# Head norms and value transposes moved into the query stage of a two-block transformer kernel on one Trainium2 core

## What is computed

```python
# block 1: local attention and pooling, then a gated FFN with a 3-tap convolution
z = rms_norm(x) @ w_in;  m = concat([attention, pool]) @ w_o;  x = x + rms_norm(m)
up = causal_dwconv(rms_norm(x) @ w_up);  y = (gelu(up_a) * up_b) @ w_down;  x = x + rms_norm(y)
# block 2: x and a context of 256 tokens, modulated by a condition vector
mods = silu(cond) @ w_ada + b_ada                       # six chunks of 2048, two for the context
kv = modulate(rms_norm(x or ctx)) @ w_in2[:, :3072]     # k_a, v_a (4 heads), k_b, v_b (8 heads)
p  = modulate(rms_norm(x)) @ w_in2[:, 3072:]            # q_a (16 heads), q_b (8 x 2), g_a, g_b
q, k = head_norm(q), head_norm(k);  both rotated (rope) for x, only normed for the context
oa = softmax(qa @ ka.T) @ va
ob = head_norm((softmax(qb0 @ kb0.T) - lam * softmax(qb1 @ kb1.T)) @ vb)
x = x + mod * ((sigmoid(g_a) * (oa @ w_br_a) + sigmoid(g_b) * (ob @ w_br_b)) @ w_out)
x = x + mod * ((silu(h @ w_ff_gate) * (h @ w_ff_up)) @ w_ff_down)
```

## Time and profile before

| what | us |
|---|---|
| runs of the kernel before | 3105.65, 3086.52, 3093.49 (median 3093.49) |
| the profiled execution, its own time | 3086.12 |
| its span, first to last instruction | 3084.3 |
| TensorE busy, weight loads aside | 2889.3 |
| VectorE, ScalarE, GpSimd busy | 1920.5, 1626.7, 806.3 |
| mean granted TensorE clock | 0.977 of 2.4 GHz |

### The profile page before, as it was taken

How to read it: one execution, slowest core, us unless ns; L and a number is a source line. 1 busy time by engine, 2 the same in 40 slices (tenths; PEclk the granted TensorE clock), 3 DMA queues, 4 the chain that set the end, 5 groups by cost and what they waited for, 6 DMA issues and landing times.

```text
span 3084.3 us, 57401 instructions
## 1 busy us (share of the span) xinstructions
PE 2889.3 (94%) x20282; PEld 2679.1 (87%) x20282; DVE 1920.5 (62%) x2324; ACT 1626.7 (53%) x2312; POOL 806.3 (26%) x646
## 2 busy tenths in 40 slices
PE   7998799899999997899999879989997999999999
PEld 7998799899999997788899769779996888888888
DVE  5566877866687766533355554657787665555554
ACT  5555566545577753323455566665555644344443
POOL 3454444403344422112242030004443400000000
PEclk9999899999999999999999889999998999999999
DMA  7873667667777775344476224348775876666665
GB/s 250 272 250 126 229 211 243 214 184 225 235 245 243 244 231 177 96 143 143 153 253 223 81 78 121 101 163 267 240 256 196 261 216 185 192 189 190 190 188 167
DMA packets 167990, 606.90 MB, mean 197 GB/s; under 512 B 18576, under 2 KB 19984, under 8 KB 167120
## 3 DMA queue, kind: packets, MB, share of 16 engines
q1 hardware_dynamic: 161856, 589.37, 60.7%
q10 hardware_dynamic: 5248, 13.30, 1.1%
q0 software_dynamic: 784, 2.88, 0.3%
HBM read 599.19 MB, written 6.29 MB: 196 GB/s over the span
## 4 chain that ended last, share of the span: by engine, by line
PE 67%; DVE 11%; ACT 9%; issue 6%; DMA 5%; ACTq 1%; DVEq 0%; SPq 0%
PE acc L1431 19%; PE acc L1427 14%; PE acc L1429 13%; PE acc L1430 12%; DVE wlo L918 4%; ACT whi L554 4%; DMA raw<-w_ada 3%; ACT cond_products L550 2%; PE acc L1419 1%; DVE conv_out L1006 1%; PE acc L1421 1%; PE acc L1422 1%; DMA raw<-w_up 1%; PE sums L1492 1%; PE acc L1639 1%
## 5 line engine op out<-in xcount | busy, mean ns | idle before, releaser
L918 DVE TENSOR_TENSOR wlo<-raw,whi 128x1024 fp32r<-128x1024 f32 x864 | 1131.7, 1319 | 952.3 <-ACT whi L554 950.6
L1431 PE MATMUL acc<-operand,wlo 128*128 128x256 f32 (+1 forms) x4992 | 1452.8, 291 | 0.0
L554 ACT ACTIVATE whi<-raw 128x1024 fp32r<-128x1024 f32 x864 | 908.5, 1057 | 942.2 <-PE acc L1431 616.1
L1429 PE MATMUL acc<-operand,whi 128*128 128x256 f32 (+1 forms) x3584 | 1073.8, 300 | 94.4 <-DVE wlo L918 58.4
L1430 PE MATMUL acc<-operand,whi 128*128 128x256 f32 (+1 forms) x3584 | 1060.4, 296 | 0.0
L1431 PEld LDWEIGHTS acc<-operand,wlo 128*128 128x128 f32 x4992 | 957.8, 192 | 15.4
L1429 PEld LDWEIGHTS acc<-operand,whi 128*128 128x128 f32 x3584 | 691.1, 193 | 124.0 <-issue 55.3
L1430 PEld LDWEIGHTS acc<-operand,whi 128*128 128x128 f32 x3584 | 691.6, 193 | 15.3 <-issue 0.2
L420 POOL TENSOR_TENSOR cond_products<-cond_products 128x512 f32<-128x512 f32 x192 | 252.6, 1316 | 1326.9 <-ACT cond_products L550 1093.1
L1427 PE MATMUL acc<-operand,whi 128*128 128x512 f32 x1408 | 495.9, 398 | 13.5 <-DVE operand L1241 7.7
L550 ACT ACTIVATE cond_products<-raw,cond_silu 128x256 f32<-128x256 f32 x768 | 327.7, 498 | 238.9 <-PE acc L1431 173.7
(11 more groups left out here) (213 smaller groups left out, 2740.1 us busy)
## 6 DMA issues: line engine op xcount, KB each, us to landing
raw<-w_ada SPq DMA_DIRECT2D x256, 512.0 KB, 4.4
raw<-w_in SPq DMA_DIRECT2D x224, 512.0 KB, 4.0
raw<-w_up SPq DMA_DIRECT2D x176, 512.0 KB, 4.4
raw<-w_down SPq DMA_DIRECT2D x88, 512.0 KB, 4.4
raw<-w_fg SPq DMA_DIRECT2D x88, 512.0 KB, 4.3
raw<-w_fu SPq DMA_DIRECT2D x88, 512.0 KB, 4.2
raw<-w_fd SPq DMA_DIRECT2D x88, 512.0 KB, 3.5
raw<-w_o SPq DMA_DIRECT2D x32, 512.0 KB, 4.4
```

Of the source, the lines that this page charges most:

```text
L554: act.activation(whi[j % RING][:], raw[j % RING][:], ACT.Copy).then_inc(hi_done, 2 if st.entries[j % st.upb - 1] == (None, ADA_VEC) else 1)
L918: dve.tensor_tensor(wlo[j % RING][:], raw[j % RING][:], whi[j % RING][:].bitcast(F32), ALU.subtract).then_inc(lo_done, 2 if prev[0] is Non ...
L1429: pe.matmul(out_, h[:, x, f], mov[:, 0], start=first, stop=False)
L1431: ins = pe.matmul(out_, l[:, x, f], mov[:, 0], start=False, stop=last)
```

## The change

- `down1`, `down2` and the query stage become `WIDE`: one 512-column matmul in place of two of 256 for each tile and half. In `down1` and q ScalarE copies the low half out (`low_half`) and VectorE adds; in `down2` VectorE does one addition more. In the last tile of a wide group the order of the two matmuls is turned around.
- up1b and up1c are one stage without conditioning; the two query stages are one (48 slots) without conditioning; gates has 8 items, glu1a 8 (of 16 groups).
- Value transposes: two groups before each of query units 1 to 6. Head norms: a list `JOBS` of chunk and slot t (query and gates slots counted through): squares at t, sums and root at t+3, inverse at t+4, broadcast and key scaling at t+7, key swap at t+9, key rotation at t+12; query chunks swap at t and rotate at t+4. The last job (chunk 11, t=50) falls into the gates stage. `broadcast` writes `TP` in place of `PS`. `swap` is 2 or 4 SBUF to SBUF DMAs on ScalarE's queue in place of 2 or 4 copies. Query rotations use tables of their own, made once.
- Gates: attention a begins at slot 7, b at 39. The values matmuls stand behind the slot's unit, not ahead of it, and all heads use one output buffer (`NB`). Gates are spilled as raw sums from two buffers, the last two kept; the sigmoid is applied after loading back.
- Output a is split in slots 56 to 63 of the gates stage, and the sums of b's squares are taken at slot 60; branch_a then takes its operand from the `who=1` half.
- GpSimd does rotation of chunk 11 between the additions of the first gates item.

```diff
-V_STEPS = {"scale": 0, "mix_out": 3, "conv": (4, 7), "down1": 0, "down2": 3, "kv": 0, "q": 0, "gate": 0,
+V_STEPS = {"scale": 0, "mix_out": 3, "conv": (4, 7), "down1": 0, "down2": 4, "kv": 0, "q": 0, "gate": 0,
            "branch_a": 0, "branch_b": 1, "out": 4, "glu": (0, 3), "down_x": 3}
-A_STEPS = {"conv": (2, 1), "glu": (2, 1)}
-WIDE = ("glu", "down_x")
+A_STEPS = {"conv": (2, 1), "glu": (2, 1), "down1": 1, "q": 1}
+WIDE = ("glu", "down_x", "down1", "down2", "q")
+LOW_FIRST = ("down1", "q")
...
-    st_up1b = Stage("up1b", pairs("w_up", "w_up", 4 * GW, DFF + 4 * GW), 8, 4, "conv", ada=1, tile0=8, feat0=8)
-    st_up1c = Stage("up1c", pairs("w_up", "w_up", 8 * GW, DFF + 8 * GW), 2 * n1 - 16, 4, "conv", tile0=16, feat0=16)
+    st_up1b = Stage("up1b", pairs("w_up", "w_up", 4 * GW, DFF + 4 * GW), 2 * n1 - 8, 4, "conv", tile0=8, feat0=8)
     st_dn1 = Stage("down1", cols("w_down", 0, 0, GW), 8, 6, "down1", ada=1, act=True, after=st_up1a)
...
-    st_q1 = Stage("q_first", cols("w_in2", 0, KVW, GW), 4, 4, "q", ada=1, tile0=8)
-    st_q2 = Stage("q_rest", cols("w_in2", 0, KVW + 1024, GW), 8, 4, "q", ada=1, tile0=32)
-    st_g = Stage("gates", cols("w_in2", 0, KVW + QW, GW), 16, 4, "gate")
-    st_ba = Stage("branch_a", cols("bra", 0, 0, GW), 8, 4, "branch_a", ada=1, op=80)
-    st_bb = Stage("branch_b", cols("brb", 0, 0, GW), 8, 2, "branch_b", per_body=4, ada=1, who=1, op=96)
+    st_q = Stage("q", cols("w_in2", 0, KVW, GW), 12, 4, "q")
+    st_g = Stage("gates", cols("w_in2", 0, KVW + QW, GW), 16, 4, "gate", ada=1)
+    st_ba = Stage("branch_a", cols("bra", 0, 0, GW), 8, 4, "branch_a", ada=1, who=1, op=80)
+    st_bb = Stage("branch_b", cols("brb", 0, 0, GW), 8, 2, "branch_b", per_body=4, ada=1, op=96)
     st_out = Stage("out", cols("out", 0, 0, GW), 8, 4, "out", ada=1, op=104)
-    st_u1a = Stage("glu1a", pairs("fg", "fu", 0, 0), 12, 4, "glu", ada=1, op=120)
...
+        def swap_at(c):
+
+            if c < NK:
+                return XC32[:, 4 + c % 2, :, 1, :]
+            return XC32[:, 6 + 2 * (c % 2):8 + 2 * (c % 2), :, 1, :]
...
+        JOBS = ((0, 1), (1, 4), (2, 7), (6, 10), (3, 13), (4, 16), (7, 19), (5, 22), (8, 26), (9, 34), (10, 42),
+                (11, 50))
+        job_at = lambda s, d: [(i, c) for i, (c, t) in enumerate(JOBS) if t + d == s]
+        job_of = {c: i for i, (c, t) in enumerate(JOBS)}
+        TURNS_A = {0: 1, 6: 2, 1: 3, 7: 4, 8: 5, 9: 6}
+        TURNS_B = {2: 1, 3: 2, 4: 3, 5: 4, 10: 5, 11: 6}
+        CH_ORDER = [c for c, t in JOBS]
+        NQ = 48
...
+                    if between is not None:
+                        between(i)
...
+            def rotate_late(c, step):
+
+                late = 3 * TURNS_B[c] - 3 + step
+                chunk, sw, dims = rotation(c)
+                cos, sin = table(c)
+                if step == 0:
+                    if c < NK:
+                        pool.wait_ge(k_swap[c % 2], swapped(c))
+                    else:
+                        pool.wait_ge(q_swap[c % 2], swapped(c))
+                        pool.wait_ge(n_sq, job_of[c] + 1)
+                    ins = pool.tensor_tensor(chunk, chunk, rep(cos, *dims), ALU.mult)
+                elif step == 1:
...
+                    pool.wait_ge(n_late, late)
+                    ins = pool.tensor_tensor(chunk, chunk, sw, ALU.add)
                 ins.then_inc(n_late, 1)
...
+            for c in (2, 3, 4, 5, 10):
+                for i in range(3):
+                    rotate_late(c, i)
+            condition_body(st_g, 0, between=lambda i: rotate_late(11, i))
+            with pool.Fori(1, st_g.bodies) as b:
...
+            def low_half(st, b, gb):
+
+                if st is st_q:
+                    tile = q_tile(2 * b + gb)
+                    act.wait_ge(v2_turned, 2 * b + gb + 1)
+                else:
+                    tile = b * (2 * st.GB) + (st.tile0 + 2 * gb + Yt)
+                act.wait_ge(used, grouped(st, b, gb))
+                act.activation(R[:, ds(tile, 2), :], PS[:, gb % 2, :, S:2 * S], ACT.Copy).then_inc(astep, 1)
...
+                    if st is st_ba and j == RING + 1:
+                        act.wait_ge(in_gb, 16)
+                        act.wait_ge(evac_done, evacuated(st_g))
+                        kept = R[:, ds(4 * b + 48, 4), :]
+                        act.activation(kept, kept, ACT.Sigmoid).then_inc(gate_b, 1)
...
+                for p in range(0, P, 2 * width):
+                    for x, y in ((p, p + width), (p + width, p)):
+                        act.dma_start(dst[x:x + width], src[y:y + width]).then_inc(
+                            (k_swap if c < NK else q_swap)[c % 2], 16)
...
+                for i, c in job_at(s, 0):
+                    if i == 0:
...
+                    if i >= 2:
+                        act.wait_ge(n_sum, i - 1)
+                    if c >= NK:
+                        act.wait_ge(evac_done, group(st_q, c - NK, 1) + 3)
+                    act.activation(sqb(i), quad(R[:, CH[c][0]:CH[c][0] + 4, :]), ACT.Square).then_inc(n_sq, 1)
+                    if c >= NK:
+                        swap(c)
+                for i, c in job_at(s, 3):
...
+                for i, c in job_at(s, 3):
+                    act.wait_ge(n_sum, i + 1)
+                    if i == 0:
+                        act.wait_ge(in_rope, 48)
+                    act.activation(HR[:, hr_cols(c)], NB[:, hr_cols(c)], ACT.Sqrt, bias=SM[:, EPS_C:EPS_C + 1],
+                                   scale=1.0 / (64 if CH[c][1] else HD)).then_inc(n_root, 1)
+                for i, c in job_at(s, 9):
+                    if c < NK:
...
+            for s in range(NQ):
+                b, j = divmod(s, st_q.upb)
+                if s + RING < NQ:
+                    hi(st_q, b, j + RING, st_q.entries[j])
+                else:
+                    hi(st_g, 0, s + RING - NQ, st_q.entries[j])
+                if j in st_q.last:
+                    low_half(st_q, b, st_q.last.index(j))
+                if 1 <= s <= 6:
+                    copy_values(2 * s - 2)
+                    copy_values(2 * s - 1)
+                norms(s)
 
...
+                if g < G_KEPT:
+                    if g == 0:
+                        act.wait_ge(n_late, 12)
+                    if g >= 2:
+                        act.wait_ge(gate_out[g % 2], 16 * (g // 2))
+                    dst = GT[g % 2]
+                else:
+                    dst = R[:, 32 + 2 * g:34 + 2 * g, :]
+                act.activation(dst, PS[:, 0, g % 2, :].rearrange("p (a n) -> p a n", a=2),
+                               ACT.Copy).then_inc(evac_done, 1)
...
+            OA_AT = {56: 0, 59: 1, 61: 2, 62: 3}
+
+            def ending(s):
+
+                if s == 56:
+                    act.wait_ge(b_summed, NB_)
+                    for x in range(2):
+                        act.dma_start(R[:, 16 + 8 * x:24 + 8 * x, :], gates[:, 8 * x:8 * x + 8, :]).then_inc(in_ga, 16)
+                if s == 57:
+                    act.wait_ge(b_out, HB)
+                    act.activation(R[:, 64:72, :], R[:, 40:48, :], ACT.Square).then_inc(o_sq, 1)
+                if s == 59:
+                    for x in range(2):
+                        act.wait_ge(gate_out[x], 16 * G_KEPT // 2)
+                    act.dma_start(R[:, 48:60, :], gates[:, 16:28, :]).then_inc(in_gb, 16)
+                if s in OA_AT:
+                    c = OA_AT[s]
+                    act.wait_ge(a_out, HA)
+                    act.activation(XC[:, 4 * c:4 * c + 4, 0, 1, :], R[:, O_SRC[c]:O_SRC[c] + 4, :],
+                                   ACT.Copy).then_inc(split_hi, 1)
+                if s == 60:
+                    act.wait_ge(o_sum, 1)
+                    for t, sums in enumerate((TP[:, 0, :], TP[:, 1, :], PS[:, 1, 0, :], PS[:, 1, 1, :])):
+                        last = act.activation(R[:, 2 * t:2 * t + 2, :], sums.rearrange("p (h n) -> p h n", h=2),
+                                              ACT.Sqrt, bias=SM[:, EPS_C:EPS_C + 1], scale=1.0 / HD)
+                    last.then_inc(o_root, 1)
+
+            s = 0
+            for b in range(st_g.bodies):
+                for j in range(RING, RING + st_g.upb):
...
+            act.wait_ge(in_ga, 32)
...
+                stored = R[:, 16 + 4 * c:20 + 4 * c, :]
+                act.activation(stored, stored, ACT.Sigmoid).then_inc(gate_a, 1)
...
+                if k in ("q", "down1"):
+                    y = R[:, ds(tile + Yt if k == "down1" else tile, 2), :]
+                    dve.wait_ge(astep, ast(st, b, gb, 0))
+                    dve.tensor_tensor(y, sums, y, ALU.add).then_inc(evac_done, 1)
...
+                        did(dve.tensor_tensor(y, y, low, ALU.add))
...
+                if s == 2:
+                    dve.wait_ge(in_rope, 48)
+                    for br in range(2):
+                        for i, col in enumerate((30, 33)):
+                            dve.tensor_scalar(XC32[:, 12 - br, i, 1, :], XC32[:, 14 + br, i, 1, :],
```

(61 more changed lines are left out.)

448 lines of the change are left out of this document (178 added, 270 removed).

## The result

The kernel after runs in 3072.91 us (median of 5 runs, 3070.48 to 3074.02) beside 3093.49 of the kernel before (5 runs, 3086.52 to 3105.65). The ratio is 0.9927, 95% interval 0.991 to 0.9943: faster by 0.7%, 20.6 us, where 48 had been forecast. One run of a later experiment (the wait of branch_a) took 3922.81 us at a granted clock of 0.673, and stands in none of its figures.

The account below looks back on a forecast made before the run. TensorE, busy 94% of the span, bounds the kernel: units at its pace plus what stands between them. Terms summed to -47.8 from the profiled 3086.1, giving 3038.3; the median lies 7.4 above: 3045 us. Range 3000 to 3090.

Parts of the forecast that it names:

- branch_a's sum: branch_a: 92.2 + 3.2 for b's squares' sums + 4 for the gates' sigmoids ahead of its loop, 99.4 us, -1.6.
- attention b: Gates slots 39 to 54: ScalarE's series chain plus conditioning products, 6.5 us a slot, 104 us; bounds 5.7 and 7.3 a slot.
- up1b: up1b without conditioning takes up1c's 92.7 us plus a 5.5 us stall from GpSimd's tree, instead of 112.9: -14.7.
- Pairs in down1 and down2: 512-column matmuls save 0.10 us a unit: down1 -5.0; down2 -4.2 and +0.7 for one more addition.
- Query stage: 48 wide units 133.4, sums and broadcasts 30.6, transposes 6.9, waits 9: 180.0 us, +16.7.
- the term of 9 for the transposes: Query stage: value transposes wait for ScalarE's copies behind `hi`, 1.7 to 1.9 us five times; bounds 0 and 11, taken 9.
- Slots 0 to 6: Gates start: units and last sums 22.0, stall near slot 5 from chunk 11's swap and rotation 8, clock 2: 32.0 us.
- rival 3: Gates conditioning served in series: products 41, scalings 15, GpSimd additions holding up VectorE 47, less 13: +90, 3135 us; chance 0.07.
- Slots 58 to 63: Gates end: 17.3 plus 3.4 for b's squares' sums and 2.6 for ScalarE; the old 7.08 us split wait goes.
- Rival 1: Whole kernel: everything is covered, the added stalls of transposes, slot 5, b, end, sigmoids and tree go: 3001 us; chance 0.20.
- rival 2: Query stage spent in waits, 3 us for each of 12 jobs: +36, 3081 us; stage over 210; chance 0.21.
- The pairs give nothing: Wide stages: the case that the change does not do what it says, 512-column pairs save nothing: +14, 3059 us.

Follow-up runs that it names:

- the wait of branch_a: Kernel after, but only branch_a's first body waits for the evacuation of the group just ahead, the others for the one before: 3058.40 us, ratio 0.9876.
- the run with plain down2: Kernel after with the four edits, but down2 without 512-column pairs and without the second addition in its evacuation: 3038.67 us, ratio 0.983.
- the run with the copies first: Kernel after, but in query slots 1 to 6 ScalarE copies the transposed values ahead of the next unit's high part: 3059.56 us, ratio 0.9882.
- the four edits: Kernel after with no turned tile, branch_a's stricter wait only in body 0, value copies before `hi`, rotation 11 in the second gates item: 3033.57 us.

## Why the prediction was wrong

The forecast was 3045 (its own sum, 3045.7, rounds to 3046), the time 3072.91. It lies inside the range of 3000 to 3090, at "same" by the 1% bound, which had a chance of 0.25. The spans differ by 13.2 us where the terms gave 47.8. The medians come out 7 us nearer to the forecast, by luck: the prediction added 7.4 us because the kernel before had been profiled in a run faster than its median, and the kernel after was profiled in its median run.

The steps that failed are, in the prediction's own terms: branch_a's sum, which had no wait at the starts of its bodies; the turned order, which had no term; the waits of the query stage, priced at their idle time; and attention b, which had the products on ScalarE in series and GpSimd's additions at nothing. The stages one by one:

**up1b.** Right: -16.7 for -14.7. The tree is still one stretch of GpSimd (10.98 us, now from 500.41), and its stall was 4.1 us (two slots of 5.44 and 4.47 in place of 2.88) for 5.5.

**Pairs in down1 and down2.** down1 right, -4.3 for -5.0. In down2 the mechanism was right and the size wrong, by the run with plain down2: about 1 us instead of 3.5. 11 of its 40 units ran at the slow spacing, and the slots at the group boundaries grew (the third from 4.37 to 5.13, the seventh from 3.39 to 3.63). The prediction carried the excess of a stage over its units across as a constant.

**Query stage.** +21.3 for +16.7. The five waits came where and as long as forecast (8.9 for 9), for the reason given, as the run with the copies first shows. The step that failed is the term of 9 for the transposes: it priced a wait at its idle time, and the removal of the waits gave 13.4. What the stage took over the forecast, 4.6, goes with the granted clock of 0.98, which is 1.00 in the run without waits.

**Gates.** -35.0 for -42.5. Slots 0 to 6 took 32.4 for 32.0, with the stall of 7.7 for 8 at its place and by its chain: the best step of the prediction, and the run that moves the rotation shows its cause. Attention a took 168.6 for 169.6, slots 55 to 57 13.7 for 13. Attention b took 107.8 for 104, and here the total hides a wrong composition: 5.1 us of every eight slots had been put down to products in ScalarE's series chain, and taking about half of their time away gave 0.9 in all sixteen. GpSimd's additions, which the forecast had at nothing and rival 3 at 47 us over the stage, give 7 to 10 in b and 4 in a. Slots 58 to 63 took 26.9 for 23.3. They hold the wait of 2.24 us ahead of branch_a's first matmul, where the prediction let the old 7.08 us go whole, and waits of 1.44 and 1.40 us for `lo`; none of them was tried.

**branch_a.** The step that failed outright: -1.6 forecast, +6.0 measured. The prediction wrote "92.2 + 3.2, and 4 for the sigmoids". Without the body waits it takes 95.6, which is 92.2 + 3.2 and leaves 0.2 for the sigmoids; with them 107.0. The stricter wait was visible in the code: `fresh` and its `+ 2` stand in the functions that the diff touches, and moving the sums away took the reason for writing body 0 out. I read the diff for what it adds, not for what its removals change.

**glu, fdown.** The other step that failed outright: forecast 0 beyond the conditioning in glu1a, measured +6.5 in fdown1, glu2 and fdown2, and 1.5 in glu1b. The prediction put the turned order at nothing without a reason: it stands in no term. The kernel before with that order alone reproduces 134.4 and 226.0. glu1a took 5.3 more for 2.8; where its other 2.5 come from was not tried.

**The sum.** Of the 34.6 us missing, branch_a is 7.6, the gates stage 7.5, the feed-forward stages behind glu1 6.5, the query stage 4.6, glu1 4.0, down2 2.8; the other stages, w_in's scatter in the main, 2.9 and down1 0.7; up1b gave 2.0 more than forecast. No single one would have made the forecast right. They are repairable: with the four edits the kernel takes 3033.57, under the forecast of 3045.

**The rivals.** Rival 1 (all covered) fell by slots 0 to 6, the transposes and b; rival 2 by the query stage's 184.6, under the 210 named. Rival 3's mechanism is real at a fraction of its price: the additions cost 10 to 14 us of the gates stage (335.3 us with small ones, 345.4 to 349.4 with full ones) where it had 47, and the half of the products' time that was taken away next to nothing where it had 41 for the whole. "The pairs give nothing" fell by down1.

## What to carry to other kernels

When a change moves a piece of work out of a loop that was written out for it, read what the loop does in its plain form: here a wait meant for the first body became one for every body and cost 11.4 us. Where TensorE runs full, price a wait above its idle time (here 1.5 times) and keep the order of matmuls the same in all tiles. Two wide and then two low ones gave one spacing, 2.79 us a unit, in the one profile of that order; the alternating order is at 2.77 at times and at 2.83 at others. A loss of 0.5% against its better case is a fair price for a time that can be relied on.

## What was not expected of the hardware

- The same stream of a 512-column and a 256-column matmul with their weight loads runs at 2.77 or at 2.83 us a unit of eight pairs at full granted clock, with nothing waited for, and keeps its spacing through whole stages (48 and 80 units). It changes only next to a slot with a wait or other matmuls in it. Turning two matmuls around in each group's last tile brings the slow one, in all of glu2 and half of fdown1; in the plain order it differs between executions and within one: down1 mostly slow (37 of 48 units) and fdown1 all fast. What decides it was not found.
- Two 512-column matmuls followed by two 256-column ones take 2.79 us a unit, in all wide stages of the one profile of that order.
- Three waits of some 2.5 us took 11.4 us of branch_a, and five of 1.7 to 2.2 took 13.4 of the query stage, by the clock granted behind them (0.94 and 0.98 of those stages).
- A VectorE instruction on one column with two inputs takes 0.16 us alone and 0.69 to 0.71 when it begins beside a GpSimd addition of 0.73: it ends with the addition. One of 1024 columns went from 1.22 to 1.51. What a meeting costs goes by what is left of the addition and not by the instruction's own length: 0.54 us for this one with 0.70 of the addition left, 0.28 for the one of 1024 columns with 0.43 left. In a chain of short instructions it weighs most.
